# Attention of tiles 2 to 4 moved beside the expert groups of tile 0, with heads in pairs

## The reference

```python
def peer_ffn(h, w_q, subkeys, u_tab, v_tab):
    def one(hc):                                   # 128 tokens
        q = (hc @ w_q).reshape(PEER_CHUNK, PEER_HEADS, 2, PEER_HALF)
        sc = jnp.einsum("chpd,pkd->chpk", q, subkeys).astype(jnp.float32)
        s_half, i_half = lax.top_k(sc, PEER_TOPK)
        ...
        top_s, top_pos = lax.top_k(cand, PEER_TOPK)
        eidx = jnp.take_along_axis(cand_idx, top_pos, axis=-1)
        gate = jax.nn.softmax(top_s, axis=-1)
        u = u_tab[eidx]
        v = v_tab[eidx]
        act = jax.nn.gelu(jnp.einsum("chkd,cd->chk", u, hc).astype(jnp.float32))
        return jnp.einsum("chk,chkd->cd", (gate * act).astype(v.dtype), v)

def trunk_layer(x, mod, lp, rope, ctx_kv):
    sh1, sc1, g1, sh2, sc2, g2 = mod
    h = rmsnorm(x, lp["norm1_g"]) * (1 + sc1) + sh1
    mix, ctx_tensors = mixer_block(h, lp, rope, ctx_kv)
    x = x + g1 * mix
    h = rmsnorm(x, lp["norm2_g"]) * (1 + sc2) + sh2
    x = x + g2 * peer_ffn(h, lp["w_peer_q"], lp["peer_subkeys"], lp["peer_u"], lp["peer_v"])
    return x, ctx_tensors
```

## Time and profile before

| | |
|---|---|
| median of 3 runs | 5584.59 us (5579.05 to 5589.23) |
| the profiled execution's own time | 5578.72 us |
| its span | 5576.9 us |
| busy share: TensorE, VectorE, ScalarE, GpSimd | 80%, 66%, 17%, 28% |
| granted clock of TensorE, mean | 0.887 |
| moved | 1585 MB, 284 GB/s over the span |

### The profile page before, as it was taken

The page is one execution under the profiler, slowest core; times in us unless marked ns, Lnnn a source line. Parts: engine busy times, 40 slices in busy tenths (PEclk is TensorE's granted clock), DMA queues, the critical chain, the costliest instruction groups (busy, mean ns, idle before and its releaser), DMA issues.

```text
span 5576.9 us, 45190 instructions
## 1 busy us (share of the span) xinstructions
PE 4439.2 (80%) x13916; PEld 2505.6 (45%) x13916; DVE 3691.8 (66%) x8036; ACT 925.0 (17%) x2668; POOL 1543.6 (28%) x1310
## 2 busy tenths in 40 slices
PE   7989898788788666666689889988887977666665
PEld 5845587444444222222268446864444432222222
DVE  1944414788777888886638453158886878888765
ACT  1132211111111111111111332011112111111111
POOL 0000000234334444445400000012333345444453
PEclk9977899899899888888889788989998988888887
DMA  4112143899988999999921111449998999999997
GB/s 163 61 68 91 46 151 136 317 355 374 377 349 346 421 421 421 421 417 422 388 85 53 68 53 63 150 157 356 360 371 348 365 373 421 421 421 421 416 422 296
DMA packets 226372, 1585.18 MB, mean 284 GB/s; under 512 B 26065, under 2 KB 28369, under 8 KB 46673
## 3 DMA queue, kind: packets, MB, share of 16 engines
q0 software_dynamic: 184320, 1342.26, 59.6%
q1 hardware_dynamic: 41808, 240.02, 11.7%
HBM read 1579.03 MB, written 3.15 MB: 284 GB/s over the span
## 4 chain that ended last, share of the span: by engine, by line
PE 39%; DMA 31%; DVE 20%; issue 4%; ACT 3%; DVEq 3%; POOL 0%; SPq 0%; ACTq 0%; POOLq 0%
DMA B<-tables,R 18%; PE ps L486 8%; PE ps L496 5%; PE ps L638 5%; DMA A<-tables,R 5%; DVE B L1485 4%; DMA H<-tables,R 4%; DVE A L1519 4%; PE ps L543 3%; PE ps L624 3%; PE ps L503 2%; PE ps L516 2%; DVE A L1485 2%; PE ps L703 2%; DMA B<-ws 2%
## 5 line engine op out<-in xcount | busy, mean ns | idle before, releaser
L486 PE MATMUL ps<-B,A 128*128 128x512 f32 x2016 | 1133.0, 704 | 494.4 <-ACT A L907 494.4
L455 POOL DMA_INDIRECT B<-tables,R x722 | 868.3, 1203 | 1889.0 <-DVEq L1469 773.4
L1485 DVE SCALAR_TENSOR_TENSOR B<-B,M 128x1024 f32<-128x1024 f32 x722 | 876.2, 1224 | 291.3 <-DMA B<-tables,R 250.6
L486 PEld LDWEIGHTS ps<-B,A 128*128 128x128 f32 x2016 | 433.8, 224 | 1131.5 <-ACT A L907 616.8
L486 PE MATMUL ps<-A 128*128 128x512 f32 x912 | 519.1, 699 | 218.0 <-ACT A L907 217.7
L496 PE MATMUL ps<-H,B 128*128 128x384 f32 (+1 forms) x2048 | 592.9, 444 | 52.0 <-DMA B<-ws 44.6
L455 POOL DMA_INDIRECT A<-tables,R x346 | 405.7, 1172 | 618.2 <-PE ps L486 397.4
L1485 DVE SCALAR_TENSOR_TENSOR A<-A,M 128x1024 f32<-128x1024 f32 x346 | 423.6, 1224 | 137.4 <-DMA A<-tables,R 113.3
L496 PEld LDWEIGHTS ps<-H,B 128*128 128x128 f32 x2048 | 399.8, 196 | 251.7 <-issue 64.4
L901 ACT ACTIVATE T<-T 128x2 f32<-128x2 f32 (+1 forms) x448 | 91.8, 205 | 2330.0 <-DVEq L1487 2329.9
L486 PE MATMUL ps<-H,A 128*128 128x512 f32 x592 | 343.1, 709 | 125.4 <-ACT A L907 125.4
(11 more groups left out here) (211 smaller groups left out, 4811.5 us busy)
## 6 DMA issues: line engine op xcount, KB each, us to landing
B<-ws SPq DMA_DIRECT2D x120, 1024.0 KB, 6.9
B<-ws SPq DMA_DIRECT2D x128, 768.0 KB, 6.1
B<-tables,R POOLq DMA_INDIRECT x722, 18.2
A<-tables,R POOLq DMA_INDIRECT x346, 15.0
R<-tabs SPq DMA_DIRECT2D x2, 2176.0 KB, 14.0
H<-tables,R POOLq DMA_INDIRECT x196, 16.4
x<-xin SPq DMA_DIRECT2D x1, 2560.0 KB, 9.3
y<-M SPq DMA_DIRECT2D x1, 2560.0 KB, 7.9
```

The lines of the kernel that those rows point to most:

```text
L455: pool.indirect_dma_start(out=ring[s], out_offset=None, in_=tables[:, :], in_offset=bass.IndirectOffsetOnAxis(ap=EI[:, n:n + 1], axis=0),) ...
L486: mm = pe.matmul(ps[:, bk + c, :], diag[PE_AT[n] % DIAGS], v_row[:, c * 512:(c + 1) * 512], start=(n % SLOTS == 0), stop=(PE_AT[n] + 1 == ...
L1485: v.scalar_tensor_tensor(out=u_row, in0=u_row, scalar=1.0, in1=h2[:, g.tile, :], op0=ALU.mult, op1=ALU.mult, accum_out=dots[:, o:o + 1])
```

## The change

Attention of tiles 2, 3 and 4 leaves its place behind tiles 0 and 1 and stands behind the queries of tiles 0 and 1. Between its units stand the first 51 groups, all of tile 0: 17 a tile, one for each of the 16 units and one at the tile's start. In these groups both slots are added on TensorE. The merge of tiles 2 to 4 then has one group a step instead of two, the queries one a step instead of two, and group 117 instead of 114 is the first of the tail.

Units of A and D alternate; two heads that lie side by side in 128 columns are turned in one transpose; ScalarE alone copies the probabilities. The exponential table of the softmax, up to 16 slots of gates (`OPENS`), and the gelu now alternate on ScalarE. The ring has six buffers at first, a seventh from slot 44; three are given back to the weights at slot 92 (`GIVEN`), and two more come when all attention is done. Since x of tiles 2 to 4 serves as workspace, it is stored and read back. The modulation's products all stand in tiles 0 and 1.

```diff
-MOD_AT = [{(None, -1): 0, (1, -1): 1, (2, -1): 2, (2, 8): 3, (3, -1): 4, (4, -1): 5}, {(None, -1): 0, (1, -1): 1, (2, -1): 2, (3, -1): 3}]
+MOD_AT = [{(None, -1): 0, (0, 4): 1, (0, 10): 2, (1, -1): 3, (1, 4): 4, (1, 9): 5}, {(None, -1): 0, (0, 5): 1, (1, -1): 2, (1, 6): 3}]
...
+ATT_STEP = UNITS + 1
+AT_MERGE = len(CHUNKS[1]) * ATT_STEP
+MG_STEP = 1
...
+KEY_STEP = 1
...
+            whole = len(out) < AT_MERGE or AT_END <= len(out) < 2 * SLOTS // 2 - 1
+            out.append(Group(t, n, size, size if whole else size - 1))
...
+EARLY = 5
+SELECTS = [(0, i) for i in range(4 * EARLY, 4 * PH)] + [(1, i) for i in range(4 * PH)]
+SELECT_AT = [q for q in range(AT_OUT) if q >= AT_MERGE or q % 3 != 2][:len(SELECTS)]
...
-LATER = {40: (5,), 132: (6,), 236: (7, 8, 9, 10, 11), 352: (12,), 400: (13,), 528: (14,)}
+FIRST = {0: "begin", 1: "queries0", 2: "queries0", 3: "queries0", 4: "queries0", 5: "queries0"}
+LATER = {44: {6: "keys0"}, 104: {7: "attention", 8: "attention"}, 200: {14: "norm1"},
+         240: {3: "queries1", 4: "queries1", 5: "queries1", 9: "queries1", 10: "queries1"}, 352: {11: "keys2"}, 400: {12: "keys3"},
+         528: {13: "keys4"}}
+GIVEN, LENT = 92, (3, 4, 5)
...
+                    if n == BLOCKS:
+                        sp.wait_ge(pe_used.sem, pe_used.at(l, PE_AT[LAST_LENT] + 1))
...
+                    elif OPENED_BY[n] == "queries0":
                         pool.wait_ge(pq_s.sem, pq_s.at(l, UNITS))
...
+                    if beside:
+                        scores(0)
                     for p in range(UNITS + 1):
-                        if p < UNITS:
-                            scores(p)
-                        if p:
-                            transposes(p - 1)
-                        if p in (5, 9, 13):
-                            values(n, t, p // 4 - 1)
+                        if beside:
+                            if p:
+                                transposes(p - 1)
+                            if p + 1 < UNITS:
+                                scores(p + 1)
...
+                        if p in (8, 16):
+                            values(n, t, p // 8 - 1, 0)
+                        if p == 9:
+                            values(n, t, 0, 1)
+                        if beside and p < UNITS:
+                            experts(l, q0 + p)
...
-                    experts(l, s * MG_STEP)
+                    if s + ROWS_0 < len(GATE_ROWS):
+                        gate_rows(s + ROWS_0)
                     mix_branch(l, 1, s)
-                    experts(l, s * MG_STEP + 1)
+                    experts(l, AT_MERGE + s)
...
+                        if beside and p < UNITS:
+                            experts(l, q0 + 1 + p)
...
                     for p in range(UNITS + 1):
-                        if p:
-                            inverse(p - 1)
-                        if p < UNITS:
-                            maxima(p)
-                        if p:
-                            pt_copy(p - 1)
+                        if beside:
+                            if p < UNITS:
+                                maxima(p)
+                                products(q0 + 1 + p)
+                                inverse(p)
+                                weighed(q0 + 1 + p)
+                        else:
+                            if p:
+                                inverse(p - 1)
+                            if p < UNITS:
+                                maxima(p)
...
+                def weighed(q):
 
                     g = GROUPS[q]
-                    products(q)
                     if g.tile and g.place == len(g.slots):
                         residual(g.tile - 1)
                     if q:
                         sums(q - 1)
                     if g.place in OPENS[g.tile]:
                         gates(g)
+                    if q in SELECT:
+                        select(*SELECT[q])
                     weights(q)
...
+                for n in CHUNKS[1]:
+                    attention(n, n - 1)
+                gate_diagonals(ROWS_0)
```

More of the change, by code:

```diff
@@ L100, in __init__, with groups @@
         self.place = first % SLOTS
-GROUPS = [Group(t, n, size, size - 1 + (164 <= n < 2 * SLOTS and (n % 4 == 2 or n >= 228))) for t in range(TILES)
-          for size in ((2, 4)[CHUNK[t]],) for n in range(t * SLOTS, (t + 1) * SLOTS, size)]
+def groups():
+    out = []
+    for t in range(TILES):
+        size = (2, 4)[CHUNK[t]]
+        for n in range(t * SLOTS, (t + 1) * SLOTS, size):
+            whole = len(out) < AT_MERGE or AT_END <= len(out) < 2 * SLOTS // 2 - 1
+            out.append(Group(t, n, size, size if whole else size - 1))
+    return out
+GROUPS = groups()
 N_GROUPS = len(GROUPS)
@@ L127, in rows_in_ring @@
     for n in range(TILES * SLOTS):
-        free[0:0] = LATER.get(n, ())
+        if n == GIVEN:
+            free = [s for s in free if s not in LENT]
+        if n in LATER:
+            free[0:0] = LATER[n]
+            fresh.update(LATER[n])
         s = free.pop(0)
         homes.append(s)
-        before.append(last.get(s))
+        opened.append(fresh.pop(s, None))
+        before.append(None if opened[-1] else last.get(s))
         last[s] = n
         free.append(s)
-    return homes, before
@@ L136 @@
-HOME, BEFORE = rows_in_ring()
+    return homes, before, opened
+HOME, BEFORE, OPENED_BY = rows_in_ring()
+LAST_LENT = max(n for n in range(GIVEN) if HOME[n] in LENT)
 TURN = [HOME[:n].count(HOME[n]) for n in range(TILES * SLOTS)]
 TURNS = [HOME.count(s) for s in range(HOMES)]
+GATE_ROWS = [(0, 0, 0), (0, 0, 1), (0, 1, 0), (0, 1, 1), (1, 0, 0), (1, 0, 1), (0, 1, 0), (0, 1, 1), (1, 1, 0), (1, 1, 1)]
+ROWS_0 = 4
 PP = {}
@@ L775, in _ @@
                 pe.wait_ge(pads.sem, pads.at(l, 2))
-                for t in range(0, TILES - 1):
-                    attention(t + 1, t)
-                values(TILES - 1, TILES - 2, 3)
+                attention(1, 0)
+                values(1, 0, 1, 1)
                 def gate_rows(i):
@@ new lines, in pt_copy @@
+                    def pt_copy(p):
+                        y, i, s = p % 2, p // 4, p // 2 % 2
+                        nb = blocks(t, y)
+                        act.wait_ge(a_t.sem, a_t.at(l, u0 + p + 1))
+                        group = 4 * n + 2 * (p // 8) + y
+                        if p % 8 < 2 and group >= 2:
+                            act.wait_ge(a_o.sem, a_o.at(l, group - 1))
+                        src = ps[:, 3:5, :].rearrange("p b n -> p (b n)")[:, 0:nb * P]
+                        act.copy(PT[y][:, 0:nb, 2 * s + i % 2, :], src.rearrange("p (i n) -> p i n", n=P)).then_inc(a_pa.sem, 1)
```

470 lines of the change are left out of this document (237 added, 233 removed).

## The result

The changed kernel takes 5498.29 us (median of 4 runs, 5494.76 to 5498.89), the kernel before 5581.82 beside it: ratio 0.9848, 95% interval 0.9831 to 0.9865. The profiled execution spans 5496.6 us, before 5576.9.

A forecast was written before the change was run, and what follows sets the result against it. No engine bounds it throughout; in the new stage VectorE and TensorE both want about 6.6 us a group. A layer: -208 - 85 - 50 - 15 + 397 = +39 us, two layers +78, so about 5660; range 5545 to 5765.

The forecast's parts named there:

- The parts of the serial stretch that go: Attention of tiles 2 to 4 leaves the serial part: 219 us, less 11 for modulation products that come back, so -208 a layer.
- the queries: Queries of tiles 2 to 4: one group a step instead of two, steps of 10 us, 50 us a layer saved.
- ScalarE binds: Rival, chance 0.09: exp-gelu switches hold ScalarE twice as long as the load shows; 8.0 us a unit, +87 a layer, 5753.
- the clock falls: Rival, chance 0.09: TensorE's clock drops to 0.84 in the new stage; 8.1 us a group, +92 a layer, 5763.
- part (2): Merge of tiles 2 to 4: one group a step instead of two, 10.4 us a step; 370 against 455, 85 saved.
- The first four steps: Start of the merge of tiles 2 to 4: stays at 76 us, each block of weights waiting for the one before.
- The new stage: 51 groups beside 48 attention units: 360 at 7.05 us a group, plus 8, 16 and 13: 397 us a layer.
- the four-buffer stretch: Last five groups beside attention, with four buffers instead of seven: 10.3 us a group instead of 7.05, 16 us more.
- The coupling: Groups beside attention: VectorE and TensorE, equally loaded, hand work to each other, so 7.05 us a group, not 6.65.
- The tail: Long last stretch, where transfers are full: 406 rows instead of 412, 6 x 2.49 = 15 us a layer saved.
- Faster: Rival, chance 0.22: engines interlock without loss, 349 us for the groups beside attention, -36 a layer, 5507 by the profiled time.
- The break-even: Groups beside attention: below 358 us for them, 7.0 us a group with everything, the change pays.

## Why the prediction was wrong

**What held.** The parts of the serial stretch that go (-204.6 for -208), and by number the queries (-51.1 for -50). That is partly luck: the 14.7 us a step of before come from a stretch that runs 40 us past the last query copy (1745.38); from copy to copy it was 12.7 in the mean, and it is 9.3 now. The forecast had both 0.4 to 0.7 too high, 13.1 and 10. In the stage the two kinds of unit, 7.1 and 5.45 us by the bare sums, measured 7.55 and 5.38. There are 192 more table loads, of 1.28 us. Rows are awaited at the start (2.9 us) and in the last groups (16.4), though for 5.8 us in between too. TensorE was to be over 85% busy at a clock of at least 0.95: it was 88 to 93% busy at 0.93, 0.97 and 0.93. The rivals in which ScalarE binds and in which the clock falls are out: without the loads the stage is 7 us shorter, and the clock of the whole stage was 0.94, where the rival had 0.84. (For each switch the Trainium skill, ScalarE: Activation LUTs, What ACT_TABLE_LOAD costs, counts 1.28 us and a drain of 1.38. The trace agrees with the first; gelu starts 1.30 us after its load did, 813.34 to 814.64, and no drain lies between.)

The forecast named as a sign of being wrong that the savings of merge and queries differ from 135 by more than 20: they were 185. The terms that failed most are the two of the merge.

**The merge's step, part (2), 21 us.** "I take 10.4 for its waits" put 0.5 on a bare sum of 9.9. TensorE is far ahead there (VectorE 6.1), and waits for 5.5 us in all from 1183 to 1449. The step is 9.46, where even the bare sum was too high, since durations of rows overlap and starts count (5.32 lasts, 5.16 to the next). Taking the row from TensorE made most steps shorter by 1.7 (7.74 from L542 to L542 above), which shows it. For the steps behind the fourth 28 x 10.4 + 3 = 294 us were forecast; they took 273 (1181.4 to 1449.0, and 5.4 ahead of the first gate). What is above 9.46 there is mostly two gate rows and one step of 15.4 us, in which ScalarE loads two tables around an exponential of gates and TensorE waits 3.15 us for its diagonal.

**The first four steps of the merge, 25 us.** "The first four steps stay at 76 us, since each block of weights still waits for the one before it to be used." They do wait, but 13.8 + 13.2 + 13.5 + 10.3 = 51. The forecast kept the price of a step whose parts all changed. From the last use of a block (the start of the row behind L503, now L540) to the first product with the next block it was 9.7, 9.3 and 9.3 us, and is 5.1, 4.5 and 4.8: 14 us less. The products of a step's first kind (L496, now L533) take 5.2 to 5.3 us from start to start instead of 6.9 to 7.2, at a granted clock of 1.00 over the four steps instead of 0.84: 7 less. A row less and a gate row more in each step are 3.5 less. VectorE's two groups a step, 13.2 us by the forecast's own sum, were not on this path: it was busy for 50 of the 76 us, and TensorE waited 0.2 us in all for a diagonal (955 to 1040). The transfers tell the same. In the merge's start of before (955 to 1034) blocks took 11.0 us to land, in that of after (1125 to 1192) 5.9; issues by count, size and median:

```profile
B<-ws SPq DMA_DIRECT2D x7, 768.0 KB, 11.0
```

```profile
B<-ws SPq DMA_DIRECT2D x8, 768.0 KB, 5.9
```

Fetching them together took the wait away. Why a block lands sooner now is not shown.

The other 3 of the 49 us are no term of the change: the forecast has 455 us for the merge before, the marks 458.

**The new stage, 26 us.** 7.05 us a group was 6.87 in the second tile (116.75 for 17, from 872.98 to 989.73), 9 us over 51 groups. The start was 6.6 (2.8 to the first copy, and the first tile's 120.6 less 116.75), not 8. The last tile lasts 135.5 to the merge's first product, so 18.8 stand for the four-buffer stretch and the end, not 16 + 13; VectorE waits 16.4 us for rows there (1060 to 1125), and giving the buffers back later removed 11 and 14, so that stretch was about right. That leaves little for the 13 of the seams and the end; what a seam costs in mid-stage is within the 6.87. The last 4 us are those that the stretch took before, which the forecast had left out. The coupling, 6.65 to 7.05, was not what I took it for: "hand work to each other within it" would have both engines pay for any added work in full. The doubled scores cost a sixth to a third of their price and the doubled maxima 0.6; one sum a group on VectorE made it busy for 58 us more and the stage 31 longer in layer 0. Where there is selection, VectorE's own sequence with its drains is nearest to being the pace, and TensorE fits in beside it.

**The tail, 11 us.** The forecast counted 6 rows fewer, by groups; but gathers that land after the last query copy are 403 instead of 412. Why three more buffers were filled by then is not shown. 412 landed in 1045.3 us, 403 in 1022.2, 2.54 us each; so 9 x 2.54 = 23, and 3 us less from the last landing to the end. This is counted in the traces and was not tried apart.

**The rival that came nearest** is Faster, 5507 us with a chance of 0.22, but by other terms than its own: it had 349 for the stage, which took 371, and 99 for the merge, which gave 134. The break-even, 358 us for the stage, was for savings of 358; with the measured ones, 204.6 + 134.2 - 1.6 + 51.1 + 26.2, it lies at 414. So that its time came near is luck. The kernel with one sum on VectorE, 31 and 38 us above the changed kernel's 371, comes close to that, and it is as fast as before.

## What to carry to other kernels

The engine that led its stage clearly ran at its bare sum, counted from start to start (9.46 us a step), so a margin for waits belongs only where two engines are near each other. There, ask for whom each one waits rather than which is busiest, and then add work to one of them alone: that decided it here. When work moves out of a stage, work out anew every wait that was sized while it was in there: the merge gave 49 us a layer more than forecast, half of it in four steps whose price had been carried over. And put a sum on the engine that has room in that stage: on TensorE beside attention (82 us of the run), on VectorE beside the merge (71 us).

## What was not expected of the hardware

TensorE's granted clock in the stage went with the work that VectorE's pace leaves it: 0.93 to 0.97 with both sums on TensorE, 0.78 with one, 0.87 with one and the scores twice, at stages of 378, 409 and 412 us; the time followed VectorE and not the clock. And 96 table loads of 1.28 us, 123 us of a stage of 378, cost 7 us.
